# Second mixer, groups 2 to 7: feature tiles by 512-column products with their halves added on VectorE; the middle groups' roots on GpSimd

## The chip, the cores and the metric

The kernel runs on one core of a Trainium2 chip, in one launch. The metric is the device time in microseconds (us). Below, PE is TensorE, DVE is VectorE, ACT is ScalarE, POOL is GpSimd, and SP issues most of the DMAs.

## The reference

`x` is 256 tokens by 1024 features, float32. Two layers run over it. Each is a half-step SwiGLU feed-forward, a token mixer, and a second feed-forward, each between two RMS norms. Layer 0 mixes with gated linear attention (GLA, 4 heads), layer 1 with the Mamba-2 mixer (SSD, 8 groups of 4 heads). The parts that the change touches, per SSD group `g`:

```python
proj = h @ w_in                                   # z, xbc, dt
xbc  = silu(causal_conv4(xbc) + conv_b)           # x: 256 features, B: 128, C: 128 of each group
wmat = (C @ B.T) * decay * dt
y    = wmat @ x + C @ state * exp(cs) + D * x
y    = y * silu(z)
y    = y * rsqrt(mean(y*y over the group's 256) + 1e-6) * g_norm
out += y @ w_out
```

GLA ends each head in the same way, with an RMS norm over the head's 256 values.

## The kernel before, in words

**Precision.** Every product is made of three. A float32 weight `w` is split into a high part (rounded to the type of the matmul) and the rest, `w = w0 + w1`, and the activations likewise, `x = x0 + x1`. The kernel sums `w0 x0 + w0 x1 + w1 x0`. ACT writes the high part of a 128x2048 block of weights (`hi`, L571), DVE subtracts it for the low part (`lo`, L1118), and `xT[:, k, 0 or 1, :]` holds both parts of x for the eight blocks of 128 input features, next to each other.

**Tiles.** A mixer projection is made per group in three blocks of 256 output columns, by slot: P1 (x of the convolution), P2 (B and C) and P3 (the gate z). P1 and P2 come out with the features on the partitions (`feature_tiles`, L1807): two tiles, each 24 products of 256 columns into a 128x256 part of a PSUM bank (L1815). P3 comes out by tokens (`token_tiles`, L1824). ACT copies a P1 or P2 tile into `feat` (L589). There DVE makes the four-tap convolution of two tiles (`convolution`: L1439 and six L1442), and ACT the silu (L928).

**Order.** Everything is written out by hand with semaphores, in order on each engine. `mixer.body(g)` projects group g, scans group g-1 and adds the output product of group g-2. Bodies 3 to 6 of SSD are a hardware loop. In such a body PE runs: P1(g), the transposes of the normed output of g-2 (L2142), transposes (L2152), P2(g), the scores (L2161, L2164), the output product of g-2 (L1761, 24 products), the state update (L2264), the products inside the chunks (L2283), the one with the state (L2287), and P3(g). P1(g) goes into the PSUM banks that hold the scan's result of the body before, so it waits on `y_out`, which DVE raises when it has read them (L1643). The transposes wait on `yn_done`, raised by the scaling of the normed output (L1531).

DVE runs in that body: `transposed` (L1548), the convolution of P1, `lo` of P3, the masked scores `wm` (L1587), the copy of the state (L1578), `lo` of P1, the convolution of P2, the output y (L1638 to L1651), `lo` of P2, `norm`, `lo` of the output weights. Body 7 (`ahead`) has the P2 convolution before the state copy, and body 2 (`second`) has it after y.

**The root.** `norm` takes the two mean squares that ACT leaves (L936, semaphore `y_sq`) and makes 1/sqrt in `rsqrt2` on DVE: an integer first guess and three Newton steps, 13 instructions on 128x1 or 128x2 elements, each waiting for the one before. The last two bodies of each mixer use ACT's square root instead (`rooted`).

**GpSimd** makes per SSD body the three side products of the scan (L516, L519, L524), one DMA, and one masking (L502).

Of the kernel before, what the change touches and what calls it, by code (L numbers as in the profile page):

```python
# [10 lines left out]
I32 = mybir.dt.int32  # L11
# [20 lines left out]
MAGIC = float(0x5F3759DF)  # L32
# [6 lines left out]
CONST_IDENT, CONST_EPS, CONST_ALL = 2, 6, 12  # L39
SSD_WEIGHTS = 4  # L40
SSD_STEPS = 15
# [26 lines left out]
def groups_before(kind):  # L68

    return 0 if kind == "gla" else GLA_H  # L70
# [94 lines left out]
def trunk(nc, x, ffn_w_gate, ffn_w_up, ffn_w_down, norm_gain, gla_w_in, gla_w_gk2, gla_b_gk,  # L165
          gla_norm, gla_w_out, ssd_w_in, ssd_conv_w, ssd_conv_b, ssd_dt_bias, ssd_A_log, ssd_D,
          ssd_norm, ssd_w_out, out):
    with ExitStack() as ctx:
# [39 lines left out]
        bcb = scr[:, 0, 1280:1664]  # L208
        zn = scr[:, 1, D:D + 512].rearrange("p (t n) -> p t n", t=NT)
# [11 lines left out]
        sm = sb("sm", [P, 48])  # L221
        ps = ctx.enter_context(nc.psum_tensor("ps", [P, 8, 512], F32))
# [64 lines left out]
        root_y = sem("root_y")  # L287

# [171 lines left out]
        def _(pool):  # L460
# [16 lines left out]
            step(pool.memset(feat[:, :, 0:CONV - 1], 0.0))  # L477
            assert step.k == CONST_ALL
# [48 lines left out]

            for b in range(NPH):
# [8 lines left out]
                if b > 0:  # L537
                    pool.wait_ge(post_read, 4 * b)
                    pool.dma_start(gpost[:, :], gain_row(2 * b + 1)).then_inc(gpost_in, 16)
                if PHASES[b][0] == "ssd":  # L540
# [14 lines left out]
                    for g in range(1, SSD_G + 1):  # L555
# [3 lines left out]
                        if g + MASKED_FIRST - 1 < SSD_G:  # L559
                            pool.wait_ge(cs_loaded[g + MASKED_FIRST - 1], 16)  # L560
                            causal(g + MASKED_FIRST - 1)


        @block.scalar
        def _(act):
# [334 lines left out]
            def mixer(ph, kind, n):  # L900
# [5 lines left out]
                def body(g, proj, scan, outp):  # L906
# [46 lines left out]
                    if proj:  # L953
                        if not ssd:
                            act.wait_ge(feat_done, 4 * (g + G))
                        tiles_out(SLOT_P1, g + n0[SLOT_P1], A,
                                  [feat[:, c, CONV - 1:] if ssd else ca[:, c, :] for c in range(2)], p1_out)
# [26 lines left out]
                    if proj and not (first and ssd):  # L984
# [6 lines left out]
                        if second:  # L991
# [3 lines left out]
                            for c in range(2, 4):  # L995
                                feature(1, c)
                        tiles_out(SLOT_P2, g + n0[SLOT_P2], 0 if first else A,
                                  [feat[:, 2 + c, CONV - 1:] if ssd else zf[:, c, :] for c in range(2)], p2_out,
                                  (1.0, 1.0) if ssd else RPRE)
# [95 lines left out]
        def _(dve):  # L1095
# [24 lines left out]

            def rsqrt2(ss, width):

                m, y, a, mh = (sm[:, o:o + 2] for o in (16, 18, 20, 22))
                step(dve.tensor_scalar(m, ss, 1.0 / width, EPS, ALU.mult, ALU.add))
                step.start(dve.tensor_scalar(mh, m, -0.5, None, ALU.mult))
                step(dve.tensor_scalar(y.bitcast(I32), m.bitcast(I32), 1, None, ALU.logical_shift_right))
                step(dve.tensor_scalar(y.bitcast(I32), y.bitcast(I32), -1.0, MAGIC, ALU.mult, ALU.add))
                for _ in range(3):
                    for o, wait in ((0, step.start), (1, step)):
                        c = slice(o, o + 1)  # L1130
                        wait(dve.scalar_tensor_tensor(out=a[:, c], in0=y[:, c], scalar=mh[:, c], in1=y[:, c],
                                                      op0=ALU.mult, op1=ALU.mult))
                    step(dve.scalar_tensor_tensor(out=y, in0=a, scalar=1.5, in1=y, op0=ALU.add, op1=ALU.mult))
                return y
# [295 lines left out]
            def convolution(g, c0, taps=range(CONV)):  # L1430


                for k in taps:
                    for j in range(2):
# [3 lines left out]
                        if k == 0:  # L1438
                            ins = dve.tensor_scalar(ca[:, c, :], src, tap, None, ALU.mult)  # L1439
# [51 lines left out]
            def mixer(ph, kind, n):  # L1491
# [11 lines left out]
                def norm(g, rooted):  # L1503
# [3 lines left out]
                    if rooted:  # L1507
# [10 lines left out]
                        step(dve.scalar_tensor_tensor(out=y, in0=a, scalar=1.5, in1=y, op0=ALU.add, op1=ALU.mult))  # L1518
                    else:
                        if not ssd:  # L1520
# [853 lines left out]
```

## Time and profile before

| | |
|---|---|
| median of 3 runs | 1087.72 us (1087.6 to 1088.41) |
| the profiled execution's own time | 1088.32 us |
| its span, first to last instruction | 1086.6 us |
| PE, DVE, ACT, POOL busy | 1075.5, 803.6, 652.9, 63.9 us |
| granted TensorE clock, mean | 0.998 of full speed |
| GLA mixer | about 211 to 300 us of the span |
| SSD mixer | about 691 to 890 us of the span |

The span begins with the first instruction. A time such as 805.29 is us from there. PE is busy for 99% of the span, but ends of matmuls are modelled, so stalls are better read from the idle column in brackets. A group of the same instruction that is drawn as one row overlaps the next row by the depth of the engine's pipeline.

### The profile page before, as it was taken

What the parts mean: (1) busy time and instruction counts of PE and PEld (TensorE: products, weight loads), DVE (VectorE), ACT (ScalarE), POOL (GpSimd) and SP (SyncE); (2) the same over time, 40 slices, a digit from 0 to 9 for tenths busy, and PEclk for the clock granted to TensorE, in tenths of its full rate; (3) what the DMA queues carried; (4) which work ended last, traced back from release to release, by engine and by line L of the source; (5) the groups of instructions that cost most, each with busy time, mean ns of one, the idle gap of its engine ahead of it and who ended that gap; (6) DMA issues with size and microseconds to landing.
All of it is one profiled execution on the core that took longest, in us unless ns stands there. A gap on an engine that the chain in (4) does not pass through costs nothing. (4 is left out here: it accounts for less than half of the span.)

```text
span 1086.6 us, 17632 instructions
## 1 busy us (share of the span) xinstructions
PE 1075.5 (99%) x6399; PEld 940.6 (87%) x6399; DVE 803.6 (74%) x1230; ACT 652.9 (60%) x1002; POOL 63.9 (6%) x85
## 2 busy tenths in 40 slices
PE   9999999999999999999999999999999999999997
PEld 7888888899888888888888888899999988888886
DVE  5867667786677666667766667899999988776664
ACT  7645446784676445457454457687777797454453
POOL 3000000000010000000000000132111111000000
PEclk9999999999999999999999999999999999999999
DMA  9874655375357555464655544595645536756531
GB/s 288 280 239 157 205 181 145 107 233 192 119 165 242 194 192 193 154 233 141 236 185 193 184 164 129 166 289 162 206 154 154 162 121 219 236 173 194 195 112 40
DMA packets 162883, 199.31 MB, mean 183 GB/s; under 512 B 6373, under 2 KB 145857, under 8 KB 162833
## 3 DMA queue, kind: packets, MB, share of 16 engines
q1 hardware_dynamic: 160288, 190.86, 54.0%
q0 software_dynamic: 2384, 7.72, 2.0%
q8 instruction: 29, 0.48, 0.2%
q14 instruction: 22, 0.17, 0.0%
q10 hardware_dynamic: 160, 0.08, 0.0%
HBM read 197.56 MB, written 1.08 MB: 183 GB/s over the span
## 5 line engine op out<-in xcount | busy, mean ns | idle before, releaser
L1211 DVE TENSOR_TENSOR ws<-raw,ws 128x1024 fp32r<-128x1024 f32 x180 | 213.3, 1222 | 139.8 <-ACT ws L657 139.8
L1761 PE MATMUL ps<-ws,hT 128*128 128x512 f32 x1320 | 314.0, 392 | 0.0
L657 ACT ACTIVATE ws<-raw 128x1024 fp32r<-128x1024 f32 x183 | 184.7, 1053 | 173.3 <-PE ps L1937 160.3
L1761 PEld LDWEIGHTS ps<-ws,hT 128*128 128x128 f32 x1320 | 243.7, 188 | 49.5 <-issue 1.1
L1923 PE MATMUL ps<-xT,ws 128*128 128x512 f32 x1152 | 267.3, 389 | 0.3 <-ACT ws L657 0.3
L1923 PEld LDWEIGHTS ps<-xT,ws 128*128 128x128 f32 x1152 | 216.1, 188 | 45.6 <-ACT ws L657 0.7
L1118 DVE TENSOR_TENSOR ws<-raw,ws 128x2048 fp32r<-128x2048 f32 (+1 forms) x88 | 197.2, 2243 | 27.8 <-ACT ws L571 27.8
L571 ACT ACTIVATE ws<-raw 128x2048 fp32r<-128x2048 f32 x83 | 157.6, 1909 | 2.7 <-PE ps L1761 2.7
L1937 PEld LDWEIGHTS ps<-xT,ws 128*128 128x128 f32 x1152 | 142.6, 192 | 2.5
L1937 PE MATMUL ps<-xT,ws 128*128 128x256 f32 x1152 | 144.1, 283 | 0.0
L1815 PE MATMUL ps<-xT,ws 128*128 128x256 f32 x960 | 119.2, 284 | 0.0
L1815 PEld LDWEIGHTS ps<-xT,ws 128*128 128x128 f32 x960 | 116.5, 192 | 0.5 <-issue 0.3
L1824 PE MATMUL ps<-ws,xT 128*128 128x256 f32 x576 | 73.5, 286 | 0.0
L1824 PEld LDWEIGHTS ps<-ws,xT 128*128 128x128 f32 x576 | 70.6, 191 | 1.0 <-issue 0.5
L1848 PE MATMUL ps<-ws,xT 128*128 128x512 f32 x240 | 57.4, 393 | 0.3 <-ACT xT L639 0.3
L1727 PE MATMUL ps<-ws,xT 128*128 128x512 f32 x240 | 56.4, 390 | 0.0
L679 ACT ACTIVATE fm<-fm 128x512 f32<-128x512 f32 x36 | 22.7, 632 | 55.2 <-DVE fm L1235 55.2
L684 ACT ACTIVATE hT<-fm 128x512 fp32r<-128x512 f32 x36 | 22.8, 632 | 51.0 <-DVE fm L1242 51.0
L1848 PEld LDWEIGHTS ps<-ws,xT 128*128 128x128 f32 x240 | 44.3, 188 | 10.0 <-issue 0.5
L1727 PEld LDWEIGHTS ps<-ws,xT 128*128 128x128 f32 x240 | 44.7, 188 | 9.1
L1247 DVE TENSOR_TENSOR hT<-fm,hT 128x512 fp32r<-128x512 f32 x36 | 24.9, 693 | 29.8 <-ACT hT L684 29.8
L673 ACT ACTIVATE ca<-ps 128x512 f32<-128x512 f32 x72 | 39.2, 597 | 12.5 <-PE ps L1937 12.5
(261 smaller groups left out, 882.0 us busy)
## 6 DMA issues: line engine op xcount, KB each, us to landing
raw<-in_ffn_w_down SPq DMA_DIRECT2D x88, 512.0 KB, 4.7
raw<-in_ffn_w_gate SPq DMA_DIRECT2D x86, 512.0 KB, 4.0
raw<-in_ffn_w_up SPq DMA_DIRECT2D x86, 512.0 KB, 5.0
raw<-in_ssd_w_in SPq DMA_DIRECT2D x48, 512.0 KB, 4.8
raw<-in_gla_w_in SPq DMA_DIRECT2D x24, 512.0 KB, 4.9
raw<-in_ssd_w_out SPq DMA_DIRECT2D x16, 512.0 KB, 4.4
raw<-in_gla_w_out SPq DMA_DIRECT2D x8, 512.0 KB, 5.1
exps<-cs_rows POOLq DMA_DIRECT2D x8, 512.0 KB, 4.8
```

The costliest lines, as they stand in the source:

```text
L571: act.activation(ws[:, slot, 0, :], raw[:, slot, :], ACT.Copy).then_inc(hi_done[slot], 1)
L657: act.activation(ws[:, 0:2, 0, c], raw[:, 0:2, c], ACT.Copy).then_inc(gu_hi, 1)
L673: act.activation(low_sums[:, 2 * s:2 * s + 2, :], ps[:, A + 2 * s:A + 2 * s + 2, T:2 * T], ACT.Copy).then_inc(low_copied, 1)
L1118: return dve.tensor_tensor(ws[:, slot, 1, cols], raw[:, slot, cols], ws[:, slot, 0, cols].bitcast(F32), ALU.subtract)
L1211: dve.tensor_tensor(ws[:, 0:2, 1, c], raw[:, 0:2, c], ws[:, 0:2, 0, c].bitcast(F32), ALU.subtract).then_inc(gu_lo, 1)
L1727: mm = pe.matmul(ps[:, bank + t, :].rearrange("p (s n) -> p s n", s=2), xT[:, k, a, t * P:(t + 1) * P], ws[:, 0:2, b, k * UW:(k + 1) * UW] ...
L1761: mm = pe.matmul(ps[:, 2 * t + n, :], hT[:, par, j, a, t * P:(t + 1) * P], ws[:, slot, b, off:off + 512], start=(first and j + a + b == 0) ...
L1815: return pe.matmul(ps[:, banks + c, 0:T], ws[:, slot, of_w, off:off + P], xT[:, k, of_x, :], start=start, stop=stop, skip_group_check=True)
L1824: return pe.matmul(ps[:, banks + t, 0:UW], xT[:, k, of_x, t * P:(t + 1) * P], ws[:, slot if home is None else home, of_w, k * UW:(k + 1) * ...
L1848: return pe.matmul(ps[:, t, :].rearrange("p (s n) -> p s n", s=2), xT[:, k, a, t * P:(t + 1) * P], ws[:, 0:2, b, k * UW:(k + 1) * UW], sta ...
L1923: pe.matmul(ps[:, A + 2 * s + j, :], weights(s, j, k, 0), xT[:, k, :, :].rearrange("p a n -> p (a n)"), start=(k == 0), stop=False, skip_g ...
L1937: mm = pe.matmul(ps[:, A + 2 * s + j, 0:T], weights(s, j, k, 1), xT[:, k, 0, :], start=False, stop=(k == KD - 1), skip_group_check=True)
```

## The change

Three things change.

1. `wide_tiles` replaces `feature_tiles` for P1 and P2 of SSD groups 2 to 7. For each of the eight blocks one product of the high weight with both parts of x, 512 columns wide, fills a whole bank, and then one of 256 columns with the low weight and the high part of x adds to the first half. A tile is 8 + 8 products instead of 24. The result is the sum of the bank's two halves.
2. ACT copies the whole 128x512 bank into one of two buffers, `halves[0 or 1]` (`halves_out`), and DVE adds the two halves into `feat` (`join`). P1 and P2 share the two buffers, so each copy first waits on `joined` for the join two tiles earlier.
3. In bodies 1 and 2 of GLA and 1 to 6 of SSD the root is made on GpSimd by `norm_root`: 6 instructions on 128x2 elements for SSD (8 for GLA), one of them a power, each waiting for the one before. DVE's `norm` waits on `root_pool` and scales.

```diff
+            def norm_root(kind, g):
+                G = groups_before(kind)
+                ss, m, y, a = (sm[:, o:o + 2] for o in (8, 16, 18, 20))
+                pool.wait_ge(y_sq, 2 * (g - 1 + G) + 2)
...
+                link(pool.tensor_scalar(m, ss, 1.0 / 256, EPS, ALU.mult, ALU.add))
+                link(pool.tensor_tensor(out=y, in0=m, in1=minus_half[:, :], op=ALU.pow))
+                link(pool.tensor_tensor(out=a, in0=y, in1=y, op=ALU.mult))
+                link(pool.tensor_tensor(out=a, in0=a, in1=m, op=ALU.mult))
+                link(pool.tensor_scalar(a, a, -0.5, 1.5, ALU.mult, ALU.add))
...
+                pool.tensor_tensor(out=y, in0=y, in1=a, op=ALU.mult).then_inc(root_pool, 1)
...
+            def halves_out(slot, count, banks, done, earlier):
+                for c in range(2):
+                    act.wait_ge(tile_mm[slot], count * 2 + c + 1)
+                    if earlier is not None:
+                        act.wait_ge(joined, earlier + c + 1)
+                    act.activation(halves[c], ps[:, banks + c, :], ACT.Copy).then_inc(done, 1)
...
+            def join(g, c, count):
+                dve.wait_ge(p1_out if c < 2 else p2_out, count + c % 2 + 1)
+                dve.tensor_tensor(feat[:, c, CONV - 1:], halves[c % 2][:, 0:T], halves[c % 2][:, T:2 * T],
+                                  ALU.add).then_inc(joined, 1)
...
-                        y = rsqrt2(ss, 256)
+                        y = sm[:, 18:20]
+                        dve.wait_ge(root_pool, g + (GLA_H - 2 if ssd else 0))
...
+            def wide_tiles(slot, banks, columns=(0, 1), free=None, low=None):
+                for c in columns:
...
+                    for k in range(KD):
+                        pe.matmul(ps[:, banks + c, :], weights(k, 0), xT[:, k, :, :].rearrange("p a n -> p (a n)"),
+                                  start=(k == 0), stop=False, skip_group_check=True)
...
+                    for k in range(KD):
+                        mm = pe.matmul(ps[:, banks + c, 0:T], weights(k, 1), xT[:, k, 0, :], start=False,
+                                       stop=(k == KD - 1), skip_group_check=True)
```

In the rows below a line number is that of the kernel it stands in. On PE, the first tile of P1 in an SSD loop body, before:

```order
L1811 REGISTER_ALU [waits y_out]
L1815 MATMUL ps<-xT,ws 128x256 [waits p2_out]
L1815 MATMUL ps<-xT,ws 128x256 x15
L1815 MATMUL ps<-xT,ws 128x256 [waits lo_done0]
L1815 MATMUL ps<-xT,ws 128x256 x7
```

And in the changed kernel:

```order
L1862 REGISTER_ALU [waits y_out]
L1867 MATMUL ps<-xT,ws 128x512 [waits p2_out]
L1867 MATMUL ps<-xT,ws 128x512 x7
L1872 MATMUL ps<-xT,ws 128x256 [waits lo_done0]
L1872 MATMUL ps<-xT,ws 128x256 x7
```

The wait on `y_out` stays where it was; 24 products become 16.

On DVE, the stretch of body 7 between `wm` and the state copy, before (L1439 and L1442 are the convolution, L1578 the copy):

```order
L1587 TENSOR_TENSOR wm<-exps,scr 128x512
L1439 TENSOR_SCALAR ca<-feat,pcol 128x256 [waits p2_out]
L1439 TENSOR_SCALAR ca<-feat,pcol 128x256
L1442 SCALAR_TENSOR_TENSOR ca<-feat,pcol,ca 128x256 [waits conv_step] x6
L1578 COPY scr<-ps 128x256 [waits upd_mm]
```

The same stretch of the changed kernel, with the rows from the body's start on (L1461 is `join`):

```order
L1582 SCALAR_TENSOR_TENSOR hT<-ps,pcol,hT 128x256 [waits yT_hi] x2
L1461 TENSOR_TENSOR feat<-scr 128x256 [waits p1_out] x2
L1475 TENSOR_SCALAR ca<-feat,pcol 128x256 [waits joined,feat_done]
L1475 TENSOR_SCALAR ca<-feat,pcol 128x256 [waits joined]
L1478 SCALAR_TENSOR_TENSOR ca<-feat,pcol,ca 128x256 [waits conv_step] x6
L1149 TENSOR_TENSOR ws<-raw,ws 128x2048 [waits hi_done2]
L1623 TENSOR_TENSOR wm<-exps,scr 128x512 [waits decay_done,e_out]
L1623 TENSOR_TENSOR wm<-exps,scr 128x512
L1461 TENSOR_TENSOR feat<-scr 128x256 [waits p2_out] x2
L1475 TENSOR_SCALAR ca<-feat,pcol 128x256 [waits joined] x2
L1478 SCALAR_TENSOR_TENSOR ca<-feat,pcol,ca 128x256 [waits conv_step] x6
L1614 COPY scr<-ps 128x256 [waits upd_mm]
```

Four joins now stand ahead of the state copy of body 7; in a loop body two stand ahead of the copy and two ahead of y.

On POOL, one body of SSD in the changed kernel (L544 to L551 are the new root; before, L519 followed L505 directly):

```order
L505 AFFINE_SELECT exps<-exps 128x1024 [waits cs_loaded5]
L544 TENSOR_SCALAR sm<-sm 128x2 [waits yn_done,y_sq]
L545 TENSOR_TENSOR sm<-sm,minus_half 128x2 [waits root_step]
L546 TENSOR_TENSOR sm<-sm 128x2 [waits root_step]
L547 TENSOR_TENSOR sm<-sm 128x2 [waits root_step]
L548 TENSOR_SCALAR sm<-sm 128x2 [waits root_step]
L551 TENSOR_TENSOR sm<-sm 128x2 [waits root_step]
L519 TENSOR_TENSOR xw<-scr,dtv 128x256 [waits tok_out]
```

The root stands between the masking of one body and the side products of the next.

## Rows read from the trace of the kernel before

**Rows 1.** The page, section 1: busy us, share of the span, instructions

```profile
PE 1075.5 (99%) x6399; PEld 940.6 (87%) x6399; DVE 803.6 (74%) x1230; ACT 652.9 (60%) x1002; POOL 63.9 (6%) x85
```

**Rows 2.** Busy times of one SSD loop body: us, engines, clock, DMA

```profile
792.00:818.31 26.31, 26.31 (x218) 24.88 (x217) 24.09 (x44) 19.34 (x35) 4.10 (x5) 1.00 0.52 162
```

**Rows 3.** Chain that ended last, within that body: start, us, what

```profile
791.64 0.43 PE ps L2264 x2
...
793.78 5.75 PE ps L1824 x48
799.53 5.76 PE ps L1815 x48
805.29 0.44 PE ps L2142 x4
```

**Rows 4.** The same view in the last feed-forward: 512-column products

```profile
942.23 7.25 PE ps L1923 x32
```

**Rows 5.** Timeline of DVE in that body: start, us, instruction [idle before]

```profile
792.11 0.42 DVE L1578 COPY scr<-ps 128x256 f32<-128x256 f32 x1 [1.42 <-PE ps L2264]
...
798.41 0.42 DVE L1643 TENSOR_TENSOR vs<-ps,dtv 128x256 f32<-128x256 f32 x1 [0.18 <-DVE yn L1638]
798.87 0.42 DVE L1646 TENSOR_TENSOR yn<-yn,vs 128x256 f32<-128x256 f32 x1
...
799.94 2.28 DVE L1118 TENSOR_TENSOR ws<-raw,ws 128x2048 fp32r<-128x2048 f32 x1
802.14 0.16 DVE L1124 TENSOR_SCALAR sm<-sm 128x2 f32<-128x2 f32 x1
...
804.55 0.62 DVE L1531 TENSOR_SCALAR yn<-yn,sm 128x256 f32<-128x256 f32 x2
...
818.42 0.43 DVE L1578 COPY scr<-ps 128x256 f32<-128x256 f32 x1 [1.66 <-PE ps L2264]
```

**Rows 6.** ACT: last square of that body, tile copy; a 512-column copy

```profile
800.77 0.19 ACT L936 ACTIVATION_READ_ACCUMULATOR scr<-yn 128x1 f32 x1
...
805.33 0.39 ACT L589 ACTIVATE feat<-ps 128x256 f32<-128x256 f32 x1 [2.49 <-PE ps L1815]
...
L673 ACT ACTIVATE ca<-ps 128x512 f32<-128x512 f32 x72 | 39.2, 597 | 12.5 <-PE ps L1937 12.5
```

**Rows 7.** Timeline of POOL, and DVE beside its third row

```profile
1.25 0.29 POOL L464 TENSOR_SCALAR_AFFINE_SELECT ident<-ident 128x128 f32<-128x128 f32 x1 [0.23 <-POOL ident L463]
1.61 0.20 POOL L467 MEMSET zr<- 128x128 f32 x1
...
754.25 2.20 POOL L516 TENSOR_TENSOR xw<-scr,dtv 128x256 f32<-128x256 f32 x1 [19.02 <-ACT scr L978]
...
807.39 0.62 POOL L516 TENSOR_TENSOR xw<-scr,dtv 128x256 f32<-128x256 f32 x1 [21.58 <-ACT scr L978]
807.97 1.04 POOL L519 TENSOR_TENSOR xdt<-scr,dtv 128x512 f32<-128x512 f32 x1
...
751.49 4.48 DVE L1118 TENSOR_TENSOR ws<-raw,ws 128x2048 fp32r<-128x2048 f32 x2
```

**Rows 8.** Timeline of PE where the loop is entered

```profile
765.68 1.15 PE L2283 MATMUL ps<-xdt,wm 128*64 128x64 f32 x32 [0.64 <-DVE wm L1587]
```

**Rows 9.** Timeline in body 7 and after it: DVE, then PE

```profile
871.22 0.41 DVE L1578 COPY scr<-ps 128x256 f32<-128x256 f32 x1
...
872.03 0.70 PE L2287 MATMUL ps<-scr,fm 128*128 128x256 f32 x2
...
880.51 1.15 PE L2283 MATMUL ps<-xdt,wm 128*64 128x64 f32 x32 [0.19 <-DVE wm L1587]
881.98 0.70 PE L2287 MATMUL ps<-scr,fm 128*128 128x256 f32 x2 [0.32 <-DVE scr L1578]
```

**Rows 10.** Timeline of GLA's first norm: last square, transposes

```profile
234.78 0.20 ACT L936 ACTIVATION_READ_ACCUMULATOR scr<-ps 128x1 f32 x1
...
242.57 0.60 PE L2142 MATMUL ps<-ident,yn 128*128 128x128 f32 x4
```

More of the change, by code:

```diff
@@ L287, in trunk @@
         root_y = sem("root_y")
+        joined = sem("joined")
+        root_step, root_pool = sem("root_step"), sem("root_pool")
         def gain_row(j):
@@ L477, in _ @@
             step(pool.memset(feat[:, :, 0:CONV - 1], 0.0))
+            step(pool.memset(minus_half[:, :], -0.5))
             assert step.k == CONST_ALL
@@ L539, in _ @@
                     pool.dma_start(gpost[:, :], gain_row(2 * b + 1)).then_inc(gpost_in, 16)
+                if PHASES[b][0] == "gla":
+                    for g in range(1, GLA_H - 1):
+                        norm_root("gla", g)
                 if PHASES[b][0] == "ssd":
@@ L955, in body @@
                             act.wait_ge(feat_done, 4 * (g + G))
-                        tiles_out(SLOT_P1, g + n0[SLOT_P1], A,
-                                  [feat[:, c, CONV - 1:] if ssd else ca[:, c, :] for c in range(2)], p1_out)
+                        if scan and ssd and not first:
+                            halves_out(SLOT_P1, g + n0[SLOT_P1], A, p1_out, None if second else 4 * (g - 2) - 2)
+                        else:
+                            tiles_out(SLOT_P1, g + n0[SLOT_P1], A,
+                                      [feat[:, c, CONV - 1:] if ssd else ca[:, c, :] for c in range(2)], p1_out)
                     def transposed(bank):
@@ L996, in body @@
                                 feature(1, c)
-                        tiles_out(SLOT_P2, g + n0[SLOT_P2], 0 if first else A,
-                                  [feat[:, 2 + c, CONV - 1:] if ssd else zf[:, c, :] for c in range(2)], p2_out,
-                                  (1.0, 1.0) if ssd else RPRE)
+                        if ssd:
+                            halves_out(SLOT_P2, g + n0[SLOT_P2], A, p2_out, 4 * (g - 2))
+                        else:
+                            tiles_out(SLOT_P2, g + n0[SLOT_P2], 0 if first else A, [zf[:, c, :] for c in range(2)], p2_out,
+                                      RPRE)
                     if scan and ssd:
@@ L1119, in low_part @@
                                          ALU.subtract)
[L1121 to L1134, printed above, removed]
             def newton(y, mh, a, last):
@@ L1559, in x_convolved @@
                     def x_convolved(between=None):
-                        dve.wait_ge(p1_out, c0 + 2)
                         dve.wait_ge(feat_done, 4 * (g + G))
-                        convolution(g, 0, range(CONV // 2))
+                        convolution(g, 0, range(CONV // 2), True)
                         if between is not None:
@@ L1566, in x_convolved @@
                         convolution(g, 0, range(CONV // 2, CONV))
+                    if proj and scan and ssd and not first:
+                        for c in range(2):
+                            join(g, c, c0)
                     if proj and not (first and ssd) and not second:
@@ L1590, in body @@
                             if ahead:
-                                dve.wait_ge(p2_out, c0 + 2)
-                                convolution(g, 2)
+                                for c in range(2, 4):
+                                    join(g, c, c0)
+                                convolution(g, 2, wide=True)
                             if second:
@@ L1624, in body @@
                         if ssd and not ahead and not first and not second:
-                            dve.wait_ge(p2_out, c0 + 2)
-                            convolution(g, 2)
+                            for c in range(2, 4):
+                                join(g, c, c0)
+                            convolution(g, 2, wide=True)
                         elif not ssd and not ahead:
@@ L1665, in body @@
                     if second:
-                        dve.wait_ge(p2_out, c0 + 2)
-                        convolution(g, 2)
+                        for c in range(2, 4):
+                            join(g, c, c0)
+                        convolution(g, 2, wide=True)
                         norm(g, tail)
@@ L2130, in body @@
                         second = ssd and isinstance(g, int) and g == 2
-                        if scan:
+                        if scan and ssd and not first:
+                            wide_tiles(SLOT_P1, A, (0, 1), (p2_out, c0 - 2), low)
+                        elif scan:
                             feature_tiles(SLOT_P1, A, (0, 1), (p2_out, c0 - 2), low)
```

43 lines of the change are left out of this document (30 added, 13 removed).

## The prediction

> **What bounds the kernel now.** First the page's busy shares [rows 1]: PE is busy for 1075.5 of 1086.6 us, so only what PE issues, or what makes PE stand, can move the end. Then the busy times of one body of the SSD loop [rows 2]: the body lasts 26.31 us and PE is busy for all of it at full clock, DVE for 24.09, ACT for 19.34, POOL for 4.10. Then the chain of waits over the same body [rows 3]: it runs through PE alone. But DVE is close behind, and that is what decides this change. I read DVE's timeline against PE's at four places.
>
> - PE takes up P1 at 799.5 [rows 3]. For that DVE must have raised `y_out`, which it does at 798.41 + 0.42 = 798.83 [rows 5]. Slack 0.5 to 0.7 us.
> - PE transposes the normed rows from 805.29 on [rows 3]. The first half is scaled at about 804.55 + 0.35 = 804.90, since two take 0.62 [rows 5]. Slack 0.2 to 0.4 us.
> - DVE stands 1.42 and 1.66 us before the state copy, waiting for PE [rows 5]. That is its reserve in the second half of a body.
> - In body 7 the copy follows the P2 convolution with no wait. It ends at 871.22 + 0.41 = 871.63, PE wants it at 872.03 [rows 9]. Slack 0.4 us.
>
> Where the loop is entered DVE is the later one: PE stands 0.64 us for `wm` [rows 8].
>
> **The change, part by part.**
>
> *Products.* 48 of 256 columns take 5.76 us, 0.120 each [rows 3]; 32 of 512 columns take 7.25, 0.2266 each [rows 4]. A pair of 256 costs 0.240, so each pair that becomes one of 512 saves 0.0134 us. A slot has 16 pairs and saves 0.21; two slots over six bodies save 12 x 0.21 = 2.6 us. The columns streamed are the same 6144 a tile: only the start costs of one instruction per pair go. The Trainium skill, "TensorE: Matmul & The Clock Gate", section "Back-to-back issue gap", gives a lone product N/2.4 + 2.5 ns; an estimate from it is 218.3 ns for the pair against 215.8, a saving of 2.5 ns. By that page this part would be 0.5 us and not 2.6. The rows differ from it, and they decide.
>
> *ACT.* A copy of 256 columns takes 0.39, one of 512 takes 0.60 [rows 6]: 24 times 0.21, 0.8 us a body. ACT has 7 us free in a body [rows 2], and the longer copy of P1's second tile still ends before PE has done its eight transposes (0.44 each four [rows 3]). Its new wait, on `joined`, holds back the weight roundings behind it, but the joins it asks for stand at least a slot earlier, or are DVE's first work in the body. I cost it at nothing; were DVE late there, ACT would pass the delay on to `hi` of P1 and P2, which have microseconds.
>
> *Joins.* A join has the form of L1646, 128x256 with two SBUF inputs: 0.42 [rows 5]. Two lie between 0.7 (overlapped) and 0.9 (end to end) us; I take 0.8. Each body has two such pairs.
>
> *Root.* DVE loses 804.55 - 802.14 = 2.41 us [rows 5] and waits for POOL instead. Behind that wait stand the output weights' `lo`, the next `transposed` and all of DVE. On POOL the new wait for `y_sq` stands ahead of the next side products, asked for at 807.39 [rows 7], which is later than the root is needed. The trace has no two-column operation on POOL and no power. Nearest rows: L464 reads and writes 128 columns, and the memset that waits for it starts 0.36 later [rows 7]. From the side products, 1.04 for 512 columns and 0.62 for 256, each column costs 1.65 ns and the rest is 0.2. So I take 0.25 per chained step, 1.5 us for six. Bounds: 0.14 a step (below L467's 0.20 with nothing added, 0.85 in all) and that of L516, 0.62 + 0.07, 4.1 in all. The power may cost more than a multiplication; I add 0.1 to 0.3.
>
> When does it begin? The squares end at 800.77 + 0.19 = 800.96, and with two joins ahead at 801.76. DVE's `lo` of P2 then runs from 800.74 to 802.95. A POOL instruction that falls under such a `lo` does not get through: L516 took 2.20 us from 754.25, ending 0.5 after the `lo` beside it (751.49 + 4.48), against 0.62 undisturbed [rows 7]. The Trainium skill, "SBUF — State Buffer", section "Who interferes with whom", says the same: a DVE instruction with two SBUF inputs and a GpSimd instruction that reads SBUF exclude each other for the whole instruction. Hence the six steps begin at 803.0, not at 801.8, and end at 804.5 to 804.8. DVE scales then, which is 0 to 0.25 later than before.
>
> *A loop body.* DVE reaches `y_out` two joins later, at 799.63, and PE's queue takes up loads and products some 0.1 after a release. P1 can start at 799.75 to 799.9 against 799.53: a stall of 0.2 to 0.4, I take 0.3. With P1 shorter by 0.21, PE reaches the transposes at 805.4, and the first scaled half is there at 805.15. No second stall. In the second half the joins cost DVE 0.8 more, against a reserve of 1.4 less PE's gain of 0.2: 0.4 is left. So a body saves 0.42 and loses 0.3: 0.1 each for the three that lie within the loop (bodies 3 to 5, to the transposes of 6), 0.3 us.
>
> *Entering the loop.* There DVE sets the pace: it loses 2.41, gains two pairs of joins (1.6), and the root is ready, since the P2 convolution lies between y and the norm in body 2. Net 0.8 earlier, of which PE can use all: its stall of 0.64 goes and 0.42 to 0.84 of products with it. Gain 0.8 us.
>
> *Body 7.* All four joins now stand ahead of the state copy. Counted from this body's transposes, the copy ends 1.6 later, at 873.2 on the old scale, while PE, with P2 shorter by 0.2, asks for it at 871.8: PE stands 1.4 and is 1.2 late. Then its own stalls of 0.19 and 0.32 [rows 9] are swallowed, since what fed them moves by 0.1 only. 1.2 - 0.5 = 0.7 is left, and P1 ahead of it adds 0.3 - 0.2. Loss 0.8 us.
>
> *GLA.* DVE loses 3 us twice, which nobody waits for. The squares end at 234.98 and PE wants the rows at 242.57 [rows 10]: 7.6 us for eight steps (2 us) and one `lo` to sit out. Nothing.
>
> *Sum:* -0.8 - 0.3 + 0.8 = -0.3 us. The profiled execution took 1088.32, 1.7 more than its span; it would become 1088.0. The runs' median is 0.6 below it, so the forecast is 1087.72 - 0.3 = **1087.4 us**. With joins at 0.7 or 0.9 a pair and the stall before P1 at 0.2 or 0.4, the likeliest case alone spans 1086.2 to 1088.8.
>
> **The rivals.**
>
> *The products' saving arrives.* If two joins overlap as closely as their elements allow, or the `y_out` wait has more slack than I read, bodies keep 0.42 each. With all of 0.64 + 0.84 at the loop's entry that is 1.5 + 3 x 0.42 = 2.8 us, less 0.3 in body 7, or 0.4 more if nothing stands there: 1085.2 to 1084.5. For it: DVE does less work in all (2.41 out, 1.6 in, per body). Against it: that gain is made late in DVE's body, the cost early, just where PE waits.
>
> *The root is late* (the other side). A scaled half later than 805.4 stops PE us for us, in four bodies (3 to 6), since transposes are in PE's one order. Up to 1.8 us of POOL chain are free. It decides at 2.4, where 4 x 0.6 takes it to 1089.8. At 3.3 us (a power of 2 us) it is 1087.4 + 4 x 1.5 = 1093.4; at the upper bound 4.1, 1087.4 + 9.2 = 1096.6. For it: nothing in the trace prices the power. Against it: the other steps are tiny.
>
> *The 512-column products bring next to nothing here*, a mechanism of the array rather than of the waits: 0.04 a slot instead of 0.21. The loop's entry still gains 0.7 (its stall), three bodies lose 0.2 each and body 7 loses 1.1. Together +1.0: 1088.7, inside the band of no change. The page on TensorE named above is the one whose gap would do this.
>
> **How the numbers follow.** No change, within 0.2% or 2.2 us, is about what a measurement of this kernel can tell. Chances: the forecast 0.47, products that bring nothing 0.05, the saving arrives 0.25, the root is late 0.23. Faster 0.25, same 0.52, slower 0.23. The range reaches into each outer rival, to 1084.6 and 1092.0, and leaves out about 2 in 10. The nearest rows of POOL set its upper end, the products' full saving its lower.
>
> **What would show it.** In the changed trace: P1 and P2 slots of 5.55 us (16 products of 512 at 0.227, 16 of 256 at 0.120); PE idle of about 0.3 before P1, released by DVE's L1681, in each loop body; POOL's six steps in about 1.5 to 1.8 us, starting when `lo` of P2 ends; DVE idle before L1565; PE idle of about 1.4 before L2346 in body 7, released by the state copy; a loop body of 26.2 us. A power above 1 us, or PE idle before the transposes L2201, makes it slower. No idle before P1 and a body of 25.9 make it faster.

## The result, and the profile after

The changed kernel takes 1089.63 us (median of 22 runs, 1089.26 to 1090.05), the kernel before beside it 1088.11 (22 runs): a ratio of 1.0013, with a 95% interval of 1.0008 to 1.0019. It is slower by 1.5 us. That is less than the 0.2% which the forecast called no change, and inside its range, but the forecast had the other sign (-0.3 us) and lies outside what was measured.

The page's first section answers [rows 1]:

```profile
PE 1075.5 (99%) x6207; PEld 931.7 (86%) x6207; DVE 798.1 (73%) x1146; ACT 658.0 (60%) x1002; POOL 89.2 (8%) x138
```

192 products fewer, DVE 5 us less busy, POOL 25 us more; and the span went from 1086.6 to 1088.3. Busy shares tell nothing of it. PE's timeline does. Here are all its rows of the changed kernel from 690 to 890 us that have idle time before them (the bracket: idle, and who ended it):

```profile
740.57 0.70 PE L2346 MATMUL ps<-scr,fm 128*128 128x256 f32 x2 [1.00 <-DVE scr L1614]
766.02 1.15 PE L2342 MATMUL ps<-xdt,wm 128*64 128x64 f32 x32 [0.35 <-DVE wm L1623]
874.08 0.70 PE L2346 MATMUL ps<-scr,fm 128*128 128x256 f32 x2 [1.25 <-DVE scr L1614]
883.72 0.70 PE L2346 MATMUL ps<-scr,fm 128*128 128x256 f32 x2 [0.25 <-DVE scr L1614]
```

L2346 reads the state copy. The 1.25 in body 7 was forecast, at 872.03 in [rows 9] there was none. The 1.00 in body 2 was not. The 0.35 answers [rows 8], where it was 0.64.

The chain of waits over a loop body answers [rows 3]:

```profile
794.03 5.75 PE ps L1881 x48
799.78 0.12 issue
799.90 2.10 PE ps L1867 x8
802.00 0.95 PE ps L1872 x8
802.95 1.84 PE ps L1867 x8
...
805.74 0.57 PE ps L2201 x4
```

The first eight 512-column products of P1 take 2.10 us, the next eight 1.84, or 0.230 each on average. So 0.26 us of the 2.10 are a wait at P1's start, with 0.12 ahead of it; the four transposes take 0.57 where [rows 3] have 0.44. DVE's timeline of the same body answers [rows 5]:

```profile
794.90 0.76 DVE L1461 TENSOR_TENSOR feat<-scr 128x256 f32<-128x256 f32 x2
...
799.34 0.42 DVE L1681 TENSOR_TENSOR vs<-ps,dtv 128x256 f32<-128x256 f32 x1 [0.18 <-DVE yn L1676]
...
805.20 0.62 DVE L1565 TENSOR_SCALAR yn<-yn,sm 128x256 f32<-128x256 f32 x2 [2.05 <-POOL sm L551]
...
808.72 1.81 DVE L1461 TENSOR_TENSOR feat<-scr 128x256 f32<-128x256 f32 x2
810.46 1.80 DVE L1475 TENSOR_SCALAR ca<-feat,pcol 128x256 f32<-128x256 f32 x2
812.18 2.46 DVE L1478 SCALAR_TENSOR_TENSOR ca<-feat,pcol,ca 128x256 f32<-128x256 f32 x6
```

`y_out` comes at 799.76 and P1 starts at 799.90. The joins are L1461: P2's take 0.76, P1's 1.81. And POOL, whose last two rows answer [rows 7]:

```profile
801.98 1.22 POOL L544 TENSOR_SCALAR sm<-sm 128x2 f32<-128x2 f32 x1 [15.75 <-ACT scr L974]
803.28 0.71 POOL L545 TENSOR_TENSOR sm<-sm,minus_half 128x2 f32<-128x2 f32 x1
804.07 0.19 POOL L546 TENSOR_TENSOR sm<-sm 128x2 f32<-128x2 f32 x1
...
804.90 0.20 POOL L551 TENSOR_TENSOR sm<-sm 128x2 f32<-128x2 f32 x1
807.88 0.62 POOL L519 TENSOR_TENSOR xw<-scr,dtv 128x256 f32<-128x256 f32 x1 [2.78 <-ACT scr L1019]
808.46 1.03 POOL L522 TENSOR_TENSOR xdt<-scr,dtv 128x512 f32<-128x512 f32 x1
```

The root sits out DVE's `lo` of P2 (it ends about 803.1) and is done at 805.10. The side products run from 807.88 on, and P1's joins, from 808.72, are beside them.

**One ruler for all kernels.** Each body holds one row of four products that scores the new keys (L2164 before, L2223 after; the line differs in the other kernels). Two rows of it in the changed kernel:

```profile
812.28 0.61 PE L2223 MATMUL ps<-fm 128*128 128x128 f32 x4
838.76 0.61 PE L2223 MATMUL ps<-fm 128*128 128x128 f32 x4
```

The distance from one to the next, 26.48 here, is a body's period. The table has these distances for every kernel, read off PE's timeline in its profiled execution: from body 1 to 2 and so on, then within body 7 (its two rows), then from there to the transposes that open the feed-forward phase behind (894.67 before, 896.41 after). The last column but one is the sum less 184.00, the sum of before; the last is the difference of the medians of the runs.

| kernel | 1-2 | 2-3 | 3-4 | 4-5 | 5-6 | 6-7 | in 7 | rest | sum | medians |
|---|---|---|---|---|---|---|---|---|---|---|
| before | 21.55 | 26.30 | 27.02 | 26.32 | 26.31 | 26.32 | 11.49 | 18.69 | 0 | 0 |
| changed | 21.14 | 27.16 | 26.66 | 26.48 | 26.48 | 26.46 | 12.82 | 18.37 | +1.57 | +1.52 |
| root on POOL only | 21.15 | 26.34 | 26.31 | 26.31 | 26.31 | 26.32 | 11.48 | 18.71 | -1.07 | -1.00 |
| wide tiles only | 21.56 | 27.45 | 28.74 | 26.75 | 26.74 | 26.79 | 12.81 | 18.38 | +5.22 | +5.65 |
| no joins | 20.97 | 26.06 | 25.97 | 25.98 | 25.97 | 25.97 | 11.49 | 18.71 | -2.88 | -2.81 |
| body 7 narrow | 21.12 | 27.17 | 26.66 | 26.48 | 26.43 | 26.64 | 11.46 | 18.89 | +0.85 | +0.90 |
| body 2 narrow | 21.12 | 26.09 | 26.59 | 26.50 | 26.44 | 26.46 | 12.82 | 18.37 | +0.39 | +0.34 |
| four halves | 21.13 | 26.79 | 26.60 | 26.59 | 26.60 | 26.46 | 12.80 | 18.38 | +1.35 | +1.46 |
| copy split in 7 | 21.12 | 27.17 | 26.66 | 26.44 | 26.46 | 26.48 | 11.49 | 19.48 | +1.30 | +1.35 |
| P2's joins behind y | 21.18 | 27.16 | 26.46 | 26.05 | 26.05 | 26.13 | 12.39 | 18.38 | -0.20 | -0.24 |
| same, behind lo too | 21.13 | 27.18 | 26.46 | 26.05 | 26.04 | 26.13 | 12.41 | 18.35 | -0.25 | -0.31 |
| that order, narrow | 21.13 | 26.33 | 26.31 | 26.31 | 26.32 | 26.31 | 11.48 | 18.72 | -1.09 | -1.10 |
| wide in 3 to 6 only | 21.14 | 26.06 | 26.43 | 26.05 | 26.05 | 26.31 | 11.48 | 18.71 | -1.77 | -1.76 |

The two last columns agree within about 0.1 us, but for one kernel (0.4: wide tiles only, of which there are 5 runs), so the stretch holds the difference: GLA and the feed-forward phases give and take nothing that shows. In single executions the start of the stretch lies between 709.99 and 710.84 us in the thirteen kernels, in no order with what they change.

### The profile page after: what moved, and what is told of

Same layout as the page of the kernel before. It is cut to its first block and busy times, and to the rows that moved or that the text cites. A ratio compares the mean times of both kernels' runs of the same rounds, so it can differ in the third digit from the quotient of the medians.

```text
span 1088.3 us, 17231 instructions
## 1 busy us (share of the span) xinstructions
PE 1075.5 (99%) x6207; PEld 931.7 (86%) x6207; DVE 798.1 (73%) x1146; ACT 658.0 (60%) x1002; POOL 89.2 (8%) x138
## 5 line engine op out<-in xcount | busy, mean ns | idle before, releaser
L1980 PE MATMUL ps<-xT,ws 128*128 128x512 f32 x1152 | 267.0, 389 | 0.0
L1980 PEld LDWEIGHTS ps<-xT,ws 128*128 128x128 f32 x1152 | 216.2, 188 | 44.9
L1994 PEld LDWEIGHTS ps<-xT,ws 128*128 128x128 f32 x1152 | 142.6, 191 | 2.5
L1994 PE MATMUL ps<-xT,ws 128*128 128x256 f32 x1152 | 144.1, 283 | 0.0
L1867 PE MATMUL ps<-xT,ws 128*128 128x512 f32 x192 | 49.1, 397 | 0.3
L1854 PE MATMUL ps<-xT,ws 128*128 128x256 f32 x384 | 47.6, 284 | 0.0
L1854 PEld LDWEIGHTS ps<-xT,ws 128*128 128x128 f32 x384 | 46.7, 192 | 0.5 <-issue 0.3
```

The source lines that it names most:

```text
L1854: return pe.matmul(ps[:, banks + c, 0:T], ws[:, slot, of_w, off:off + P], xT[:, k, of_x, :], start=start, stop=stop, skip_group_check=True)
L1867: pe.matmul(ps[:, banks + c, :], weights(k, 0), xT[:, k, :, :].rearrange("p a n -> p (a n)"), start=(k == 0), stop=False, skip_group_check ...
L1980: pe.matmul(ps[:, A + 2 * s + j, :], weights(s, j, k, 0), xT[:, k, :, :].rearrange("p a n -> p (a n)"), start=(k == 0), stop=False, skip_g ...
L1994: mm = pe.matmul(ps[:, A + 2 * s + j, 0:T], weights(s, j, k, 1), xT[:, k, 0, :], start=False, stop=(k == KD - 1), skip_group_check=True)
```

## The experiments

The theory: DVE's joins eat more than everything else brings. Rivals: the root on POOL is late or in the way; the 512-column products bring less than [rows 4] say.

**1. Root on GpSimd only** (`norm_root` kept; tiles, copies and convolutions as before):

```diff
-                        if scan and ssd and not first:
+                        if scan and ssd and not first and not ssd:
                             wide_tiles(SLOT_P1, A, (0, 1), (p2_out, c0 - 2), low)
...
-                            for c in range(2, 4):
-                                join(g, c, c0)
-                            convolution(g, 2, wide=True)
+                            dve.wait_ge(p2_out, c0 + 2)
+                            convolution(g, 2)
```

> The middle roots on GpSimd alone: tiles, copies and convolutions are those of before, nothing is joined. Theory 1 (VectorE's joins are the cost, the root on GpSimd is harmless): the stall of 0.64 us at the loop's entry goes, since VectorE is 2.4 us lighter there; in a loop body the root is ready about 0.3 us before VectorE used to scale, so nothing stands; 0.5 to 0.7 us faster than before, about 1087.5. Theory 2 (the root on GpSimd comes too late and its chain is in the way of the side products): slower than before by about 1 us, 1089, with PE idle ahead of the transposes or of the state product.

Measured: 1087.12, ratio 0.9992 (0.9983 to 1.0001). The interval just touches 1, but the periods are plain: 0.40 less from body 1 to 2, 0.71 less from 3 to 4, nothing elsewhere. The second is the stall of [rows 8], where DVE is the later one. The first is this row of before, which I had not looked at; ACT (the silu) released it, after a wait for DVE's convolution:

```profile
731.03 0.91 ACT L928 ACTIVATE fm<-ca,pcol 128x256 f32<-128x256 f32 x2 [0.69 <-DVE ca L1442]
...
732.09 0.30 PE L2161 MATMUL ps<-ident,fm 128*128 128x128 f32 x1 [0.25 <-ACT fm L928]
```

By the ends of the single products in the trace that product of before comes 0.55 us after the one ahead of it, and 0.11 in this kernel: that is the 0.40. Neither place has idle time here. The root on POOL alone makes nothing wait, so the rival "root is late" falls as the main cause.

**2. Wide tiles only** (the changed kernel with DVE's `rsqrt2` back):

```diff
-                        y = sm[:, 18:20]
-                        dve.wait_ge(root_pool, g + (GLA_H - 2 if ssd else 0))
+                        y = rsqrt2(ss, 256)
```

> The 512-column products, copies and joins alone, every root on VectorE as before. Theory 1: nothing pays for the joins now; about 1.3 us more at the loop's entry, PE idle about 0.3 us before P1 and some 0.7 before the transposes in each loop body, body 7 as in the changed kernel: 1091 to 1094. Theory 2: without the chain on GpSimd the products' saving of 2.6 us shows: 1086 to 1087.

Measured: 1093.77, ratio 1.0054 (1.0040 to 1.0068). Two rows of its PE timeline, `wm` in body 3 and the transposes in body 7:

```profile
767.73 1.15 PE L2356 MATMUL ps<-xdt,wm 128*64 128x64 f32 x32 [1.89 <-DVE wm L1637]
861.72 0.63 PE L2215 MATMUL ps<-ident,yn 128*128 128x128 f32 x4 [0.29 <-DVE yn L1579]
```

At the loop's entry 1.89 us, where the changed kernel has 0.35. The chain of waits in a loop body, which runs through PE alone before, here goes through DVE's root and scaling to the transposes:

```profile
807.70 0.36 DVE yn L1579
808.11 0.70 PE ps L2215 x4
```

The root on POOL saves the changed kernel 3.7 us by the periods, 4.1 by the medians. That is three to four times what it is worth alone, since with the joins DVE is the later engine in the loop bodies too.

**3. No joins.** PE works all its products, but ACT copies only 256 columns into the feature tile, without its wait on `joined`. The kernel leaves out `w0 x1`, so it only serves to price things:

```diff
-                    if earlier is not None:
-                        act.wait_ge(joined, earlier + c + 1)
-                    act.activation(halves[c], ps[:, banks + c, :], ACT.Copy).then_inc(done, 1)
+                    act.activation(outs[c], ps[:, banks + c, 0:T], ACT.Copy).then_inc(done, 1)
...
-                dve.tensor_tensor(feat[:, c, CONV - 1:], halves[c % 2][:, 0:T], halves[c % 2][:, T:2 * T],
-                                  ALU.add).then_inc(joined, 1)
```

> The changed kernel, but ScalarE copies only the first 256 columns of the product straight into the feature tile, and nothing is joined; this leaves the weight's high part times x's low part out of the feature tiles of groups 2 to 7, PE works the same products. Theory 1: 3 us faster than the changed kernel, 1086.5, loop body of 25.9 us, no idle before P1, none of 1.25 before the state product of body 7. Theory 2 (root): within 0.5 of the changed kernel, and VectorE still idle 2 us for the root with PE late behind it. Theory 3 (a 512-column product is dearer than two of 256 inside this loop): body of 26.3 or more, although nothing waits.

Measured: 1085.31, ratio 0.9975 (0.9966 to 0.9984), 4.3 us under the changed kernel and not 3. The chain of waits in a loop body (P1's first tile, then the transposes):

```profile
797.41 1.84 PE ps L1861 x8
799.25 0.95 PE ps L1866 x8
...
803.00 0.44 PE ps L2195 x4
```

No wait at P1, transposes back at 0.44, body 25.97. And DVE, where P1's joins stood before:

```profile
805.67 1.39 DVE L1469 TENSOR_SCALAR ca<-feat,pcol 128x256 f32<-128x256 f32 x2
806.98 4.01 DVE L1472 SCALAR_TENSOR_TENSOR ca<-feat,pcol,ca 128x256 f32<-128x256 f32 x6
```

Without joins the taps lie beside the side products, and they stretch instead: 5.32 us from 805.67 to 810.99. In the changed kernel joins and taps take 5.92, from 808.72 to 814.64. P1's joins cost DVE 0.6 us, not 1.81; the wait for GpSimd is there either way. But whoever waits for the joins alone gets them a microsecond late.

This kernel prices both sides. Against "root on POOL only" the products save 26.31 - 25.97 = 0.34 us a body, 1.81 in all and not 2.6. A tile's eight 512-column products take 1.84, which is 0.230 each on average, but that is no steady pace. By the ends of the single products in the trace the first five of most tiles follow at 0.233, 0.234, 0.228, 0.234 and 0.231 us, the rest at 0.2267. The 24 of the output product in the same body begin alike and go on at 0.2267, and the 32 of [rows 4], which stand behind other 512-column products, have 0.2267 from the first to the last. So each run of 512-column products behind narrower ones costs about 0.026 us at its start, 24 tiles 0.6 us. Another 0.2 stays in body 2, where PE comes sooner to a wait before the transposes (0.42 from one end to the next, 0.24 in "root on POOL only").

Against the changed kernel the joins with the longer copies and ACT's waits cost 4.45: 1.10 in body 2, 0.69 into body 3, 0.50 in each loop body, 1.33 - 0.34 in body 7, and 0.17 before all these. (-1.07 - 1.81 + 4.45 = +1.57.) The Trainium skill, "TensorE: Matmul & The Clock Gate", section "Back-to-back issue gap", gives N/2.4 + 2.5 ns for a lone product, by which 512 columns would take 215.8 and 256 columns 109.2; an estimate of the saving from these is 2.5 ns a pair. Here the products of a tile, each with its own weights, follow at 230 and 119 ns on average, and the rows decide. Two products made one save 10 ns in a tile of eight (0.240 by [rows 3], less 0.230; 32 pairs a body make 0.32 of the 0.34), not 13.4 as I had it.

**4. Body 7 narrow** (in `mixer` of all three engines):

```diff
-                        if scan and ssd and not first:
+                        if scan and ssd and not first and not ahead:
                             wide_tiles(SLOT_P1, A, (0, 1), (p2_out, c0 - 2), low)
```

> The changed kernel, with body 7's tiles P1 and P2 as before (256-column products, two plain copies, no joins). Theory 1: the idle of 1.25 us before body 7's state product goes, 0.4 us of products come back: 0.8 to 1.2 us faster than the changed kernel, 1088.5 to 1088.8. Theory 2: the stall stays, within 0.3 us of the changed kernel.

Measured: 1089.02, ratio 1.0010 (1.0001 to 1.0019), 0.6 to 0.7 us under the changed kernel, a little less than theory 1 had. The 1.25 us are gone (12.82 to 11.46), but the stretch behind is longer by 0.52 and the one before by 0.18. A stall at 874 hides the smaller ones of [rows 9]; take it away and they are back.

**5. Copy split in body 7.** The joins stay, only DVE's order changes:

```diff
-                                convolution(g, 2, wide=True)
+                                convolution(g, 2, range(CONV // 2), True)
+                                state_copied()
+                                convolution(g, 2, range(CONV // 2, CONV))
```

> The changed kernel with body 7's state copy put between the second and third tap of P2's convolution instead of behind the fourth. If the stall of 1.25 us there is the four joins ahead of the copy: the copy comes 1.6 us earlier, the stall is gone, 1.0 to 1.3 us faster than the changed kernel, 1088.3 to 1088.6. Rival: the state product's operands are late in another way (wm, ScalarE), and the stall moves to the products of wm: no gain.

Measured: 1089.45, ratio 1.0012 (1.0003 to 1.0021). Neither outcome as I put it. The stall is gone, and PE's timeline shows what took its place:

```profile
880.16 0.63 PE L2204 MATMUL ps<-ident,yn 128*128 128x128 f32 x4 [0.47 <-DVE yn L1565]
881.54 1.15 PE L2345 MATMUL ps<-xdt,wm 128*64 128x64 f32 x32 [0.31 <-DVE wm L1623]
883.01 0.70 PE L2349 MATMUL ps<-scr,fm 128*128 128x256 f32 x2 [0.32 <-DVE scr L1614]
```

1.10 us in three pieces for 1.50 in two. DVE works through the end of the mixer as one chain; moving the joins within it moves the wait along.

**6. Body 2 narrow** (the edit of experiment 4 with `not second`; a `memset` raises `joined` by the four that body 2's joins would have given).

> The changed kernel with body 2's tiles P1 and P2 as before. If the joins of body 2 make the stall of 1.00 us there and the 0.35 us before wm in body 3: both go, 0.17 of products comes back twice: 0.9 to 1.1 us faster than the changed kernel, 1088.6. Rival: the stall of 1.00 us is the root's or the side products': it stays.

Measured: 1088.47, ratio 1.0002 (0.9993 to 1.0011), 1.2 us under the changed kernel. The 1.00 us are gone, 27.16 to 26.09, but of the 0.35 us before `wm` in body 3 0.29 are left. What is left goes when body 3 has no joins either (experiment 3); of its own joins only P1's stand ahead of `wm`. They were not taken out by themselves.

**7. Four halves.** Why does body 2 stand 1.00 us? ACT and DVE in the changed kernel there:

```profile
731.67 0.60 ACT L627 ACTIVATE scr<-ps 128x512 f32<-128x512 f32 x1 [0.27 <-DVE feat L1461]
732.85 0.60 ACT L627 ACTIVATE scr<-ps 128x512 f32<-128x512 f32 x1 [0.58 <-DVE feat L1461]
...
730.94 1.82 DVE L1461 TENSOR_TENSOR feat<-scr 128x256 f32<-128x256 f32 x2
733.86 2.80 DVE L1623 TENSOR_TENSOR wm<-exps,scr 128x512 f32<-128x512 f32 x2 [1.11 <-ACT scr L1045]
```

P1's joins take 1.82 us beside the side products; ACT's P2 copies wait for them, since there are two buffers for four halves; the copy of the scores (L1045) stands behind those on ACT; `wm` waits for it, and the state copy stands behind `wm`. With four buffers ACT need not wait:

```diff
-        halves = [scr[:, 1, o:o + 512] for o in (512, 1536)]
+        flat = scr[:, :, :].rearrange("p a n -> p (a n)")
+        halves = [scr[:, 1, o:o + 512].rearrange("p (a n) -> p a n", a=2) for o in (512, 1536, 1024)]
+        halves.append(flat[:, 1664:2944].rearrange("p (a n) -> p a n", a=2)[:, :, 0:T])
...
-                            halves_out(SLOT_P2, g + n0[SLOT_P2], A, p2_out, 4 * (g - 2))
+                            halves_out(SLOT_P2, g + n0[SLOT_P2], A, p2_out, None if second else 4 * (g - 2) - 2, 2)
```

> The changed kernel with four buffers for the copied halves, so that ScalarE's copies of P2 no longer wait for the joins of P1 (the first square's scratch and the P2 halves use free columns of scr and vs). If that wait, which the prediction cost at nothing, makes the stall of 1.00 us before the state product in body 2: the two waits of 0.27 and 0.58 us go, the stall falls by 0.5 to 0.8 and the kernel by as much, 1088.9 to 1089.1. Rival (the joins themselves, 1.81 us beside GpSimd's side products, make VectorE late): the stall stays within 0.2 us, no change from the changed kernel. Loop bodies stay at 26.47 in both.

Measured: 1089.56, ratio 1.0014 (1.0005 to 1.0023), no different from the changed kernel as a whole. But body 2 did what was expected, on DVE and on PE:

```profile
732.66 1.71 DVE L1625 TENSOR_TENSOR wm<-exps,scr 128x512 f32<-128x512 f32 x2 [0.40 <-ACT scr L1047]
...
739.39 0.70 PE L2348 MATMUL ps<-scr,fm 128*128 128x256 f32 x2 [0.30 <-DVE scr L1616]
```

0.70 of the 1.00 us went, but the period from 2 to 3 is only 0.37 shorter, and those from 4 to 5 and 5 to 6 are 0.11 and 0.12 longer. The chain of waits in a loop body shows where (the first tile of P2):

```profile
805.36 0.44 PE ps L2213 x4
805.79 1.98 PE ps L1869 x8
```

1.98 where the changed kernel has 1.84. P2 goes into the banks of P1 and so waits for ACT's copy of P1's second tile. That copy starts 0.21 us after the tile's last product in bodies 4 to 6, where the changed kernel has 0.04, and 0.40 after it in body 3 (0.11 there), where P2 begins 0.30 later. Why ACT starts later I did not find; the buffers lie otherwise in SBUF too, and ACT writes one of them with a stride.

**8. P2's joins behind y** in bodies 3 to 6 (ACT takes the squares and P3's copies ahead of P2's features):

```diff
-                        if ssd and not ahead and not first and not second:
-                            for c in range(2, 4):
-                                join(g, c, c0)
-                            convolution(g, 2, wide=True)
-                        elif not ssd and not ahead:
+                        if not ssd and not ahead:
...
+                    if ssd and proj and not ahead and not first and not second:
+                        for c in range(2, 4):
+                            join(g, c, c0)
+                        convolution(g, 2, wide=True)
                     if proj and not ahead:
                         lo(SLOT_P2, g + n0[SLOT_P2] + 1)
```

> The changed kernel with one order changed in bodies 3 to 6: VectorE does y first, then the joins and the convolution of P2, then lo of P2 and the norm; ScalarE takes the squares and P3's copies ahead of P2's features. If the joins are dear because they stand ahead of y_out: no idle before P1, loop body 25.97 us as with no joins at all, VectorE's idle of 2 us for the root gone, body 7's stall down from 1.25 to about 0.6: 2.0 to 2.5 us faster than the changed kernel, 1087.1 to 1087.6. Rival: the root's steps fall among the convolution's products, which hold GpSimd off, and end behind lo of P2, so that the transposes wait: as slow as the changed kernel or slower.

> As the run before it, with lo of P2 ahead of the joins and the convolution of P2. The root then starts when lo ends and runs beside the joins and taps. If GpSimd gets through between VectorE's short instructions, the norm comes as early as in the run before it, but ScalarE has P2's features 2.3 us later, which holds its next copies of P1: between equal to the run before it and 0.5 us a body slower. If not, the root ends only with the convolution and both are alike.

Measured: 1087.86, ratio 0.9999 (0.9989 to 1.0008), and with `lo` ahead of the joins 1087.79, 0.9996 (0.9987 to 1.0005). 1.8 us under the changed kernel, body 26.05. So the joins are dear by their place, not by their length: DVE does all four here too. P1 waits no more. Against "no joins" a body keeps 0.08, and the chain of waits has it in P2's first tile, 1.91 for 1.84:

```profile
805.01 0.44 PE ps L2215 x4
805.45 1.91 PE ps L1871 x8
```

That is PE waiting for ACT's copy of P1's second tile, now 512 columns (0.60 us for 0.39). In the changed kernel's loop bodies the late transposes hide it. The edit moves P2's whole convolution on DVE and three things on ACT together, and no run separates the two. The root, and DVE beside it, in the first of the two:

```profile
798.71 0.83 POOL L546 TENSOR_TENSOR sm<-sm,minus_half 128x2 f32<-128x2 f32 x1
799.62 0.19 POOL L547 TENSOR_TENSOR sm<-sm 128x2 f32<-128x2 f32 x1
799.89 2.52 POOL L548 TENSOR_TENSOR sm<-sm 128x2 f32<-128x2 f32 x1
...
800.07 2.28 DVE L1165 TENSOR_TENSOR ws<-raw,ws 128x2048 fp32r<-128x2048 f32 x1
803.07 0.62 DVE L1569 TENSOR_SCALAR yn<-yn,sm 128x256 f32<-128x256 f32 x2 [0.71 <-issue]
```

The steps get through among the taps of the convolution; the one that meets `lo` takes 2.52 us instead of 0.19. The two orders give the same time.

**9. That order with narrow tiles** (the control: the root on POOL, no join, P2's convolution behind y).

> The roots on GpSimd with narrow tiles everywhere, and P2's convolution behind y in bodies 3 to 6: the order of the run late_conv without a join. The trace of the same kernel in the old order shows no idle of PE in those bodies, so the order alone gives nothing: 26.31 us a body, 1086.9 to 1087.4. If it is faster than that, part of what late_conv won did not come from the joins.

Measured: 1087.03, ratio 0.9988 (0.9979 to 0.9998), the periods of "root on POOL only" to 0.02. The order alone is worth nothing; in experiment 8 it won back what the joins had cost.

**10. The version that beats both:** root on GpSimd, wide tiles in bodies 3 to 6, that order there:

```diff
-                        if scan and ssd and not first:
+                        if scan and ssd and not first and not ahead and not second:
                             wide_tiles(SLOT_P1, A, (0, 1), (p2_out, c0 - 2), low)
...
+                        dve.wait_ge(p2_out, c0 + 2)
+                        dve.memset(sm[:, 24:25], 0.0).then_inc(joined, 4)
+                        convolution(g, 2)
```

> Wide tiles in bodies 3 to 6 alone, bodies 2 and 7 as before, the roots on GpSimd, and P2's joins and convolution behind y in bodies 3 to 6. From the periods of the runs so far: from body 1 to 2 21.15 us and from 2 to 3 26.34 as with narrow tiles and the root on GpSimd, then four bodies of 26.0 to 26.1 as with P2's joins late, body 7 and the tail 11.5 and 18.7 as before. Beside before that is -0.4 + 0 - 1.0 - 3 x 0.27 = -2.2 us: 1085.9. If it is 1087.1 or more (the root on GpSimd alone), wide tiles are worth nothing even there.

(The `memset` gives `joined` the four of body 2.) Measured: 1086.37, ratio 0.9982 (0.9973 to 0.9991): 1.8 us under before and 3.3 under the changed kernel, and 0.5 short of what was expected. Body 3 kept one stall that I had counted as gone:

```profile
764.57 1.15 PE L2353 MATMUL ps<-xdt,wm 128*64 128x64 f32 x32 [0.32 <-DVE wm L1631]
```

The other miss is the period from 6 to 7, which I had put at 26.05 and which holds the narrow tiles of body 7: 26.31, as before. Of the 1.76 us, 1.1 are the root's; wide tiles bring 0.7.

## Why the prediction was wrong

- **Entering the loop** is the step that failed. Forecast -0.8 ("0.8 earlier, of which PE can use all"); the first three periods of the table give -0.41 + 0.86 - 0.36 = +0.1. The gain at the two places where DVE is late came, 0.77 us of it. The loss of 0.86 in body 2 was not in the sum. I looked at DVE's net work up to the stall that before has and never asked what stands in body 2, where before has none. With the tiles of body 2 narrow it is gone (experiment 6).
- **ACT's wait on `joined`: "I cost it at nothing".** The text says that the joins asked for are "DVE's first work in the body". They are, and in body 2 that is too late: 0.70 of that body's 1.00 us of idle hang on this wait (experiment 7, whose period became 0.37 shorter).
- **ACT's longer copy "still ends before PE has done its eight transposes".** Not quite. P2's first product waits for it 0.08 us in a loop body where the transposes are in time (experiment 8). In bodies 2 and 3 of the changed kernel ACT comes to it late, and by the ends of the products P2 starts 0.15 and 0.14 late there.
- **Joins, 0.8 a pair.** 0.76 for P2's. 1.81 for P1's, which lie beside the side products; I had seen what the lock costs on POOL's side [rows 7] and did not apply it to DVE's new instructions. DVE's own load hardly changes by it (experiment 3); what changes is when the joins are done, and ACT waits for just that. The Trainium skill, "SBUF — State Buffer", section "Who interferes with whom", says that it holds both ways, and the 1.81 and the 2.52 of experiment 8 agree.
- **Products, 2.6 us.** 1.81 came: mis-sized, since 0.2266 was read from runs of 32 and a tile has runs of eight, each behind narrower products, with 0.026 us more at its start (0.6 us in all); another 0.2 goes into a wait in body 2 (experiment 3). The average of 0.230 is only 1.5% more, but that is a quarter of a difference between two such numbers.
- **A loop body, -0.1.** Measured +0.16. The stall before P1 was forecast at 0.3 and is 0.38, with `y_out` at 799.76 (forecast 799.63); the products give 0.34 for 0.42; and the transposes start 0.13 late, where the forecast said "no second stall". Three bodies: +0.47 instead of -0.3.
- **Body 7, +0.8.** Right in mechanism, place and nearly in size: a stall of 1.25 (forecast 1.4), partly offset by the smaller ones that it swallows; +1.33 - 0.32 = +1.0.
- **Root.** Right that it waits out the `lo` of P2. From the end of `lo` it takes 2.0 us, not 1.5 to 1.8, as the power adds 0.5 and not 0.1 to 0.3. It is ready at 805.10, 0.3 after the forecast's upper end, and with the joins ahead of it that is 0.13 late for the transposes; without joins nothing waits. Its own gain alone, 1.1 us, is more than the 0.64 of [rows 8], by the 0.40 between bodies 1 and 2.
- **GLA, nothing.** Right, as far as single executions show: PE has no idle row there, before or after.

The errors were all on one side, and add up: 0.9 at the entry, 0.8 in the loop, 0.2 at the end, 1.9 us against a forecast of -0.3.

## What to carry over

Halving a product's count pays by the difference of two pitches, and what puts the halves together pays by where it stands: price the second first, at every point where an engine has under 1 us of reserve, and not only at the stalls that the old trace shows. When two changes meet in one kernel, run each alone: here one was a gain of 1.0 and the other a loss of 5.6 (5.2 by the periods), and together they looked like almost nothing. They do not add up either: beside the joins the first is worth 3.7 to 4.1. Before a step is called late or cheap, try it elsewhere in its engine's order; with P2's two behind y, four joins and their longer copies cost 0.08 us a body (26.05 to 25.97) instead of 0.50. And a price read from the middle of a long run of equal instructions leaves out what a short run pays at its start.

## What the runs showed that was not expected

- GpSimd takes 0.19 to 0.20 us for an operation on two columns and 0.27 to 0.28 from one chained step to the next, but 0.69 to 1.00 for a power on two columns (0.71 in the loop body shown).
- Two 256-column sums on VectorE take 0.76 us alone and 1.81 beside GpSimd's products (0.62 to 1.03 each). In the same way a two-column step on GpSimd took 2.52 us instead of 0.19 beside one `lo` of 2.28.
- 512-column products with new weights each follow one another at 0.2267 us in a long run, in this loop and in the feed-forward phase alike. Behind narrower products the first five take 0.226 to 0.236, 0.026 us more together, so that a run of eight takes 1.84 us and not 1.81; behind other 512-column products [rows 4] there is no such start.
